# Two PSUM banks for the projections of mixer A, their evacuations two steps later, and one score bank fewer

## The chip, the cores and the metric

The kernel runs on all 8 cores of one Trainium2 chip, each core on 1024 of the 8192 tokens, with no exchange between cores. The time is the device time of the slowest core in microseconds (us); a result is the median over executions.

## The reference, cut to what matters

The program is one layer of a hybrid encoder: RMSNorm, a combined input projection, mixer A (dilated sliding-window attention, 8 heads of 128), mixer B (grouped-query attention over all tokens), an output projection, a product-key expert layer, and a last norm. The change touches mixer A alone:

```python
h = rms_norm(x, norm1_g[l])
proj = h @ w_in[l]
qa, ka, va, qb, kb, vb = jnp.split(proj, splits, axis=-1)
out_a = dilated_window_attention(qa_, ka_, va_)
...
# in dilated_window_attention, for each block of queries and three (window, dilation) branches:
sc = jnp.einsum('bhqd,bhqpkd->bhqpk', qblk, kg).astype(jnp.float32) * scale
sc = sc + bias[None, :, None]          # ALiBi
p = jnp.exp(sc - lse[..., None])
o = jnp.einsum('bhqpk,bhqpkd->bhqpd', p.astype(v.dtype), vg)
w = jax.nn.softmax(lse, axis=-1)       # the branches are joined by their denominators
```

The kernel computes it as one dense attention over a window of 3072 tokens, where a precomputed mask holds how often a key is hit by the branches, times the exponential of the ALiBi term.

## The kernel before, in words

Every operation goes through a small recorder (class Fw). Each engine executes its operations in the order in which they were recorded, and waits for the operations on which its own depend, by the names in r= and w=. ("ps", b) is PSUM bank b, of which there are eight (0 to 3 in psA, 4 to 7 in psB). There is no planner: the order of record is the order of execution.

The stages are: norm of the window, query projection of mixer B (bank 0, 1), mixer A, keys and values of mixer B, attention B, output projection, expert layer (the largest), last norm. A barrier of all engines stands between stages, so a stage starts when the one before has ended.

Mixer A works head by head. a2_loads (L374) fetches a head's weights WA and its mask. a2_proj_groups (L379) cuts a head's projections into 14 groups, each of which fills a bank of 128x512: six groups for the keys (L401, 16 matmuls of 512 columns), two for the queries (L407, the same) and six for the values (L414, 64 matmuls of 128 columns). A group of keys or queries is cut in four pieces of 4 matmuls, one of values in four pieces of 16: 56 pieces a head. All go to bank 0. Keys and queries are evacuated by ScalarE (L403, L410), values by VectorE (L417), and the evacuation is recorded right behind the last piece of its group.

Head 0's projections run alone, ahead of all attention. Those of head h+1 run between the steps of head h's attention, through hook: it is called once in each of a head's 40 steps (two chunks of 20 key tiles, one for each 512 queries), and records as many pieces as bring their count to 1.4 times the steps so far, so the steps bring 2, 1, 2, 1, 1 pieces, and so on. Head 7 has no projections beside it.

attention (L276 ff) with three score banks (sbanks 1, 2, 3) works with a lookahead of L = 2. Step i records on TensorE the scores qk(i+2) (L285, one matmul of 512 columns), on ScalarE the exponential of step i (L296), on VectorE the mask product of step i (L301), on TensorE pv(i) (L310 and L311: values and denominators, two matmuls of 512 columns), and then calls hook. At a chunk's end VectorE takes the reciprocal of the denominators (L315) and multiplies (L316). Mixer B uses the same function, with four banks and without mask and hook.

The lines that set the rhythm:

```python
L = nb - 1
...
if i + L < n:
    qk(i + L)
...
fw.op("pe", pv, r=[pid, vid, "ones"], w=[("ps", pso), ("ps", psd)])
if hook is not None:
    hook(i)
```

Of the kernel before, what the change touches and what calls it, by code (L numbers as in the profile page):

```python
# [10 lines left out]
BF16 = mybir.dt.bfloat16  # L11
U32 = mybir.dt.uint32
AF = mybir.ActivationFunctionType
# [112 lines left out]
def build_program():  # L126
    nc = bass.Bass("TRN2", target_bir_lowering=False)
    fw = Fw()
# [61 lines left out]
    ar = Ar()  # L190
# [84 lines left out]

    def attention(KT_fn, V_fn, QT, kts, kid, vid, qid, mask_fn, mask_id, E2, P2, rec, dst, dst_id, pso, psd, tagc,  # L276
                  sbanks=(2, 3), hook=None):
# [42 lines left out]
    hwin = ar.alloc([128, 16, WIN], BF16)  # L320
# [6 lines left out]
    for ck in range(WIN // 256):  # L327
        s = ck % 2
# [19 lines left out]
    win_ids = [("hwin", i) for i in range(6)]  # L348
    for tt in range(8):
        for half in range(2):  # L350
            def mm(e, tt=tt, half=half):
                ins = None
                for dk in range(16):
# [5 lines left out]
                                                           func=AF.Copy), r=[("ps", half)], w=["qraw"])  # L359
# [5 lines left out]
    WA = [ar.alloc([128, 16, 384], BF16) for _ in range(2)]  # L365
    maskS = [ar.alloc([128, 23, 128], BF16) for _ in range(2)]
    KT_h = [ar.alloc([128, WIN], BF16) for _ in range(2)]
    V_h = [ar.alloc([128, 24, 128], BF16) for _ in range(2)]
    QT_h = [ar.alloc([128, TOK], BF16) for _ in range(2)]
    E2 = [ar.alloc([128, 512], BF16) for _ in range(3)]  # L370
    P2 = [ar.alloc([128, 512], BF16) for _ in range(3)]
    rec = ar.alloc([128, 512])

    def a2_loads(h):  # L374
        s = h % 2
        fw.dma("gp", WA[s], wA[h].rearrange("(dk p) c -> p dk c", p=128), w=[("WA", s)])
        fw.dma("sp", maskS[s].rearrange("p a b -> p (a b)"), maskA[h], w=[("mask", s)])

    def a2_proj_groups(h):  # L379
        s = h % 2  # L380
        pieces = []

        def add_group(nmm, mk_mm, evac):
            per = 4 if nmm == 16 else 16
            for p0 in range(0, nmm, per):
                last = (p0 + per >= nmm)

                def piece(p0=p0, last=last):
                    def mm(e):
                        ins = None  # L390
                        for q in range(p0, p0 + per):
                            ins = mk_mm(e, q)
                        return ins
                    fw.op("pe", mm, r=[("WA", s)] + win_ids, w=[("ps", 0)])
                    if last:
                        evac()
                pieces.append(piece)

        for c6 in range(6):
            add_group(16,  # L400
                      lambda e, dk, c6=c6: e.matmul(bank(0), WA[s][:, dk, 128:256], hwin[:, dk, c6 * 512:(c6 + 1) * 512],  # L401
                                                    start=(dk == 0), stop=(dk == 15)),
                      lambda c6=c6: fw.op("act", lambda e: e.activation(out=KT_h[s][:, c6 * 512:(c6 + 1) * 512], in_=bank(0),  # L403
                                                                         func=AF.Copy), r=[("ps", 0)], w=[("KTh", s)]))
        for c2 in range(2):
            add_group(16,
                      lambda e, dk, c2=c2: e.matmul(bank(0), WA[s][:, dk, 0:128],  # L407
                                                    hwin[:, dk, 1024 + c2 * 512:1024 + (c2 + 1) * 512],
                                                    start=(dk == 0), stop=(dk == 15)),
                      lambda c2=c2: fw.op("act", lambda e: e.activation(out=QT_h[s][:, c2 * 512:(c2 + 1) * 512], in_=bank(0),  # L410
                                                                         func=AF.Copy), r=[("ps", 0)], w=[("QTh", s)]))
        for gg in range(6):
            add_group(64,
                      lambda e, q, gg=gg: e.matmul(bank(0)[:, (q // 16) * 128:(q // 16 + 1) * 128],  # L414
                                                   hwin[:, q % 16, (4 * gg + q // 16) * 128:(4 * gg + q // 16 + 1) * 128],
                                                   WA[s][:, q % 16, 256:384], start=(q % 16 == 0), stop=(q % 16 == 15)),
                      lambda gg=gg: fw.op("dve", lambda e: e.tensor_copy(  # L417
                          V_h[s][:, 4 * gg:4 * gg + 4, :].rearrange("p a b -> p (a b)"), bank(0)),
                          r=[("ps", 0)], w=[("Vh", s)]))
        return pieces  # L420

    a2_loads(0)
    for g in a2_proj_groups(0):
        g()
    for h in range(8):
        s = h % 2
        if h + 1 < 8:
            a2_loads(h + 1)
            pend = a2_proj_groups(h + 1)
        else:  # L430
            pend = []
        cnt_t = [0]
        npend = len(pend)

        def hook(i, pend=pend, cnt_t=cnt_t, npend=npend):
            cnt_t[0] += 1
            want = (npend * cnt_t[0] + 39) // 40
            while pend and (npend - len(pend)) < want:
                pend.pop(0)()
        for qc in range(2):  # L440
            kts = list(range(4 * qc, 4 * qc + 20))
            qt0 = 8 + 4 * qc
            pso, psd = (4, 5) if qc == 0 else (6, 7)

            def mask_fn(i, kts=kts, qt0=qt0, s=s):
                m0 = 11 - (kts[i] - qt0)
                return maskS[s][:, m0:m0 + 4, :].rearrange("p a b -> p (a b)")
            attention(lambda kt, s=s: KT_h[s][:, kt * 128:(kt + 1) * 128], lambda kt, s=s: V_h[s][:, kt, :],
                      QT_h[s][:, qc * 512:(qc + 1) * 512], kts, ("KTh", s), ("Vh", s), ("QTh", s), mask_fn, ("mask", s),
                      E2, P2, rec, mixA[:, h, qc * 512:(qc + 1) * 512], ("mixT", h), pso, psd, "A",  # L450
                      sbanks=(1, 2, 3), hook=hook)
        while pend:
            pend.pop(0)()
    fw.barrier()

    ar.p = P0
# [145 lines left out]
    mixB = ar.alloc([128, 8, TOK], BF16)  # L602
    E2 = [ar.alloc([128, 512], BF16) for _ in range(4)]
    rec = ar.alloc([128, 512])
    cnt = 0
    for h in range(8):
        kv = h // 4
        for qc in range(2):
# [18 lines left out]
    for oc in range(4):  # L627
        s = oc % 2
        fw.dma("gp", Wo[s], w_out3[:, :, oc * 512:(oc + 1) * 512], w=[("Wo", s)])
        for tt in range(8):  # L630
            b = k % 4
            k += 1

            def mm(e, tt=tt, s=s, b=b):
# [8 lines left out]
                r=[("ps", b), "acc"], w=["acc"])  # L643
# [15 lines left out]
    for tt in range(8):  # L659
# [33 lines left out]
    for piece in range(4):  # L693
        s = piece % 2
        fw.dma("gp", Wq[s], wq3[:, :, piece * 512:(piece + 1) * 512], w=[("Wq", s)])
        for bb in range(4):
            blk = piece * 4 + bb
            for half in range(2):
                b = k % 4
                k += 1  # L700

                def mm(e, bb=bb, half=half, s=s, b=b):
# [7 lines left out]
                    out=qT[:, blk, half * 512:(half + 1) * 512], in_=bank(b), func=AF.Copy), r=[("ps", b)], w=["qT"])  # L710
# [11 lines left out]
    pb = ar.alloc([128, 128], U32)  # L722
# [160 lines left out]
    for tt in range(8):  # L883
        onehot_prelude(tt)
        nxt = topk_stages(tt + 1) if tt + 1 < 8 else []
        for g in range(128 // NT):
            if g < len(nxt):
# [3 lines left out]
               r=[("Gs", tt % 2, tq_) for tq_ in range(0, 128, 4)], w=[("Gd", tt)], key=("Gdk", tt % 2))  # L891
# [10 lines left out]
           w=["acc"] + [("acc", t_, o_) for t_ in range(8) for o_ in range(4)], key="accld")  # L902
# [3 lines left out]
    for grp in range(128 // GRP):  # L906
        gsl = grp % 2
        for j in range(GRP):
# [5 lines left out]
                   r=all_gd, w=[("Gc", s3)])  # L914
            for half in range(2):
                b = kU % 2
                kU += 1

                def mm(e, s3=s3, half=half, b=b):
# [9 lines left out]
                    r=[("ge", b), ("Gc", s3)], w=[("AT", gsl, j)])  # L929
        for tt in range(8):  # L930
            for oc in range(4):
                b = 4 + (kV % 4)
                kV += 1

                def vm(e, gsl=gsl, tt=tt, oc=oc, b=b):
# [8 lines left out]
                    r=[("ps", b), ("acc", tt, oc)], w=[("acc", tt, oc)], extra=None)  # L944
# [11 lines left out]
    for tt in range(8):  # L956
        s = tt % 2
# [7 lines left out]
              r=[("rsf", tt), "gf"], w=[("ost", s)])  # L965
# [82 lines left out]
```

How the kernel before makes its waits and increments, by code:

```python
            def body(e, mine=mine, final=final):  # L103
                seen = {}
                for o in mine:
                    for j in sorted(o["deps"]):
                        k, v = self.ops[j]["sig"]
                        if seen.get(k, 0) >= v:
                            continue
                        seen[k] = v
                        e.wait_ge(sems[k], v)
                    if o["fn"] is None:
                        continue
                    ins = o["fn"](e)
                    if o["signal"]:
                        k, v = o["sig"]
                        ins.then_inc(sems[k], 16 if o["dma"] else 1)
                if final is not None:
                    for k, v in sorted(final.items(), key=str):
                        if k[0] == "k" and seen.get(k, 0) < v:
                            e.wait_ge(sems[k], v)
```

## Time and profile before

| | us |
|---|---|
| median of 3 runs | 5597.22 (5590.62 to 5888.88) |
| profiled execution, its own time | 5602.27 |
| profiled execution, span of the slowest core (core 2) | 5600.7 |
| spans of all cores | 5557.3 to 5600.7 |
| mixer A on core 2: projections of head 0 | 442.6 to 506.7 |
| mixer A on core 2: attention of heads 0 to 7 | 506.7 to about 1320 |
| TensorE busy over the span | 3926.2 (70%) |
| VectorE busy over the span | 2332.9 (42%) |
| ScalarE busy over the span | 1555.9 (28%) |

The profile is of one execution, on the slowest core. Every position below is in us from the start of the span. PE is TensorE's matmuls, PEld its weight loads, DVE is VectorE, ACT is ScalarE. The ends of matmuls are modelled: those of a row of matmuls overlap the next start, so the distance of two starts is the time that a matmul takes of the engine, and a listed idle time is shorter than the pause between them by the overlap.

### The profile page before, as it was taken

The page shows a single profiled execution, that of the slowest core. Times are in us where ns is not written, and L with a number is a line of the kernel's source. Part 1 is how long each engine was busy: PE and PEld are TensorE (multiplying, and loading weights), DVE is VectorE, ACT ScalarE, POOL GpSimd, SP SyncE. Part 2 cuts the span into 40 slices and gives each one's busy share as a digit, 9 for nine tenths or more (in the row PEclk, how much of TensorE's full clock was granted, in tenths as well). Part 3 has the DMA queues.
Part 4 walks back from the last instruction along what each step waited for, and adds up shares of the span by engine and source line. Part 5 has one row for each costly group of instructions (what it writes and reads, how often), then busy time and mean ns, then how long its engine had stood idle before and what let it go on. Part 6 is the DMA issues. An engine that isn't in the chain of part 4 may idle for free.

```text
span 5600.7 us, 66235 instructions; the slowest of 8 cores (5557.3 to 5600.7 us)
## 1 busy us (share of the span) xinstructions
PE 3926.2 (70%) x21336; PEld 1894.4 (34%) x21336; DVE 2332.9 (42%) x4103; ACT 1555.9 (28%) x2416; POOL 509.6 (9%) x359
## 2 busy tenths in 40 slices
PE   1246777775666999968631111139999999999997
PEld 1113444342333444423211111114444444444443
DVE  4341333334333010002069899835353444444444
ACT  2111222224666888851212121110100000000001
POOL 0000000000000000000014444420000000000000
PEclk8568999997888999989765555569999999999998
DMA  5302011004553000034400100154545445454544
GB/s 136 79 0 45 18 31 21 17 7 116 168 160 98 1 1 1 1 82 106 64 1 30 60 31 30 60 150 82 100 89 94 95 89 100 85 104 80 109 76 115
DMA packets 306814, 382.78 MB, mean 68 GB/s; under 512 B 139440, under 2 KB 262704, under 8 KB 302896
## 3 DMA queue, kind: packets, MB, share of 16 engines
q0 software_dynamic: 72240, 168.35, 17.1%
q1 hardware_dynamic: 234240, 210.21, 13.2%
q8 instruction: 182, 2.98, 0.2%
q14 instruction: 152, 1.25, 0.1%
HBM read 496.52 MB, written 50.33 MB: 98 GB/s over the span
## 4 chain that ended last, share of the span: by engine, by line
PE 66%; DVE 12%; issue 7%; ACT 5%; DMA 5%; POOL 3%; another core or an unknown queue 1%; DVEq 0%; ACTq 0%; SPq 0%; POOLq 0%
PE psB L938 16%; PE psA L922 16%; PE psB L310 6%; PE psB L311 5%; PE psA L285 5%; PE psA L521 3%; PE psA L401 3%; PE psA L414 3%; DVE arena L862 2%; DMA arena<-xT 2%; PE psA L705 2%; PE psA L637 2%; POOL arena L864 2%; PE psA L354 1%; DVE arena L860 1%
## 5 line engine op out<-in xcount | busy, mean ns | idle before, releaser
L922 PE MATMUL psA<-arena 128*128 128x512 bf16 x4096 | 893.1, 380 | 55.1 <-DMA arena<-UT_l 47.1
L938 PE MATMUL psB<-arena 128*128 128x512 bf16 x4096 | 889.2, 379 | 43.8 <-DVE arena L927 43.8
L296 ACT ACTIVATE arena<-psA 128x512 bf16<-128x512 f32 x1344 | 778.7, 599 | 306.6 <-PE psA L285 257.6
L942 DVE TENSOR_TENSOR arena<-psB,arena 128x512 f32<-128x512 f32 x1024 | 706.6, 691 | 212.8 <-PE psB L938 211.4
L310 PE MATMUL psB<-arena 128*128 128x512 bf16 x1344 | 516.5, 384 | 171.1 <-DVE arena L301 165.1
L926 ACT ACTIVATE arena<-psA 128x512 bf16<-128x512 f32 x256 | 152.8, 597 | 1641.3 <-PE psA L922 1622.2
L872 PE MATMUL psB<-arena 128*128 128x128 bf16 x1024 | 133.5, 303 | 647.6 <-POOL arena L864 545.2
L922 PEld LDWEIGHTS psA<-arena 128*128 128x128 bf16 x4096 | 401.3, 98 | 541.5 <-issue 60.9
L938 PEld LDWEIGHTS psB<-arena 128*128 128x128 bf16 x4096 | 398.5, 98 | 534.5 <-issue 58.6
L311 PE MATMUL psB<-arena 128*128 128x512 bf16 x1344 | 516.5, 384 | 0.0
L285 PE MATMUL psA<-arena 128*128 128x512 bf16 x1344 | 502.1, 383 | 1.0 <-DVE arena L584 1.0
L927 DVE TENSOR_TENSOR arena<-arena 128x512 bf16<-128x512 bf16 x256 | 108.9, 425 | 854.9 <-ACT arena L926 769.8
L315 DVE RECIPROCAL arena<-psB 128x512 f32<-128x512 f32 x32 | 107.4, 3356 | 635.5 <-PE psB L311 635.5
L301 DVE SCALAR_TENSOR_TENSOR arena<-arena 128x512 bf16<-128x512 bf16 x320 | 223.8, 746 | 301.3 <-ACT arena L296 299.1
L872 PEld LDWEIGHTS psB<-arena 128*128 128x128 bf16 x1024 | 94.1, 132 | 686.9 <-issue 677.9
L877 ACT ACTIVATE arena<-psB 128x512 bf16<-128x512 f32 x256 | 139.0, 595 | 631.4 <-PE psB L872 631.2
L864 POOL TENSOR_TENSOR arena<-arena 128x2048 bf16<-128x2048 f32 x64 | 265.4, 4146 | 452.7 <-DVE arena L862 434.1
L310 PEld LDWEIGHTS psB<-arena 128*128 128x128 bf16 x1344 | 132.4, 99 | 364.8 <-issue 234.8
L521 PE MATMUL psA<-arena 128*128 128x512 bf16 x768 | 207.3, 435 | 41.4 <-ACT arena L528 37.7
L401 PE MATMUL psA<-arena 128*128 128x512 bf16 x768 | 207.3, 408 | 35.5 <-DMA arena<-wA 19.6
L41 POOL DMA_DIRECT2D arena<-UT_l x128 | 67.8, 530 | 1689.6 <-PE psA L922 1671.7
L414 PE MATMUL psA<-arena 128*128 128x128 bf16 x3072 | 194.1, 219 | 18.0 <-DVE arena L417 11.3
(147 smaller groups left out, 3414.4 us busy)
## 6 DMA issues: line engine op xcount, KB each, us to landing
arena<-xT SPq DMA_DIRECT2D x44, 2048.0 KB, 13.3
arena<-UT_l POOLq DMA_DIRECT2D x128, 512.0 KB, 7.3
arena<-V_l POOLq DMA_DIRECT2D x128, 512.0 KB, 9.6
Gd<-arena SPq DMA_DIRECT2D x8, 4096.0 KB, 11.6
arena<-Gd SPq DMA_DIRECT2D x128, 256.0 KB, 10.5
arena<-wA POOLq DMA_DIRECT2D x8, 1536.0 KB, 11.7
arena<-x_own SPq DMA_DIRECT2D x1, 8192.0 KB, 35.0
arena<-w_out POOLq DMA_DIRECT2D x4, 2048.0 KB, 27.9
```

The source lines that it names most:

```text
L285: fw.op("pe", lambda e, kt=kt, b=b: e.matmul(bank(b), KT_fn(kt), QT, start=True, stop=True), r=[kid, qid], w=[("ps", b)])
L296: fw.op("act", lambda e, b=b, Eb=Eb: e.activation(out=Eb, in_=bank(b), func=AF.Exp, scale=SCALE), r=[("ps", b)], w=[("E", i % nb)])
L310: e.matmul(bank(pso), V_fn(kt), Pb, start=(i == 0), stop=(i == n - 1))
L311: return e.matmul(bank(psd), ones_bf, Pb, start=(i == 0), stop=(i == n - 1))
L401: lambda e, dk, c6=c6: e.matmul(bank(0), WA[s][:, dk, 128:256], hwin[:, dk, c6 * 512:(c6 + 1) * 512], start=(dk == 0), stop=(dk == 15)),
L414: lambda e, q, gg=gg: e.matmul(bank(0)[:, (q // 16) * 128:(q // 16 + 1) * 128], hwin[:, q % 16, (4 * gg + q // 16) * 128:(4 * gg + q // 16 ...
L521: ins = e.matmul(bank(bb), xb[s][:, dk, sub * 128:(sub + 1) * 128], Wkv[:, dk, :], start=(dk == 0), stop=(dk == 15))
L864: fw.op("gp", lambda e: e.tensor_tensor(A1[s], A1t[s], RT[:, 2, t0:t0 + NT].unsqueeze(2).to_broadcast([128, NT, 128]), ALU.mult), r=["RT", ...
L872: ins = e.matmul(bank(b)[:, j * 128:(j + 1) * 128], A1[s][:, 4 * q4 + j, :], A2[s][:, 4 * q4 + j, :], start=True, stop=True)
L922: ins = e.matmul(bank(b), UT[s3][:, dk, :], h2T[:, dk, half * 512:(half + 1) * 512], start=(dk == 0), stop=(dk == 15))
L938: ins = e.matmul(bank(b), AT[gsl][:, j, tt * 128:(tt + 1) * 128], Vc[gsl][j][:, oc * 512:(oc + 1) * 512], start=(j == 0), stop=(j == GRP - 1))
L942: fw.op("dve", lambda e, tt=tt, oc=oc, b=b: e.tensor_tensor(acc[:, tt, oc * 512:(oc + 1) * 512], bank(b), acc[:, tt, oc * 512:(oc + 1) * 5 ...
```

## The change

Projections alternate between banks 0 and 1, by the number of the group in its head (pb). Each piece now comes as a pair of the piece and, for the last of a group, its evacuation. In the attention of a head, hook does not record the evacuation behind its piece: it puts it on the list late, with the present step plus 2, and records it at the start of the call of hook in that step, ahead of that step's pieces. What is left on the list when the head's attention has been recorded is recorded then, behind the last reciprocal and product. Head 0's own projections are evacuated at once as before, but in alternating banks. Bank 1 was a score bank: mixer A's attention has two, (2, 3), which makes L = 1, and two buffers each for E2 and P2 in place of three.

```diff
-    E2 = [ar.alloc([128, 512], BF16) for _ in range(3)]
-    P2 = [ar.alloc([128, 512], BF16) for _ in range(3)]
+    E2 = [ar.alloc([128, 512], BF16) for _ in range(2)]
+    P2 = [ar.alloc([128, 512], BF16) for _ in range(2)]
...
+        gcount = [0]
 
         def add_group(nmm, mk_mm, evac):
             per = 4 if nmm == 16 else 16
+            pb = gcount[0] % 2
+            gcount[0] += 1
...
-                    fw.op("pe", mm, r=[("WA", s)] + win_ids, w=[("ps", 0)])
-                    if last:
-                        evac()
-                pieces.append(piece)
+                    fw.op("pe", mm, r=[("WA", s)] + win_ids, w=[("ps", pb)])
+                pieces.append((piece, (lambda pb=pb: evac(pb)) if last else None))
...
     a2_loads(0)
-    for g in a2_proj_groups(0):
-        g()
+    for (pc, ev) in a2_proj_groups(0):
+        pc()
+        if ev is not None:
+            ev()
...
+        late = []
+
+        def hook(i, pend=pend, cnt_t=cnt_t, npend=npend, late=late):
             cnt_t[0] += 1
+            for (d, ev) in [x for x in late if x[0] <= cnt_t[0]]:
+                ev()
+            late[:] = [x for x in late if x[0] > cnt_t[0]]
             want = (npend * cnt_t[0] + 39) // 40
             while pend and (npend - len(pend)) < want:
-                pend.pop(0)()
+                pc, ev = pend.pop(0)
+                pc()
+                if ev is not None:
+                    late.append((cnt_t[0] + 2, ev))
...
-                      sbanks=(1, 2, 3), hook=hook)
+                      sbanks=(2, 3), hook=hook)
         while pend:
-            pend.pop(0)()
+            pc, ev = pend.pop(0)
+            pc()
+            if ev is not None:
+                late.append((0, ev))
+        for (d, ev) in late:
+            ev()
+        late[:] = []
```

The matmuls and evacuations of the groups are the same as before, with bank(pb) for bank(0).

## Rows read from the trace of the kernel before

**Rows 1.** The page, chain that ended last, shares of the span by line

```profile
PE psB L938 16%; PE psA L922 16%; PE psB L310 6%; PE psB L311 5%; PE psA L285 5%; PE psA L521 3%; PE psA L401 3%; PE psA L414 3%; DVE arena L862 2%; DMA arena<-xT 2%; PE psA L705 2%; PE psA L637 2%; POOL arena L864 2%; PE psA L354 1%; DVE arena L860 1%
```

**Rows 2.** Stretches (PE, PEld, DVE, ACT, POOL, PEclk, DMA): a head; later stage

```profile
613.69:722.72 109.03, 83.29 (x632) 46.12 (x632) 39.44 (x52) 26.18 (x49) 1.14 (x2) 0.94 0.13 22
...
1330.00:1640.00 310.00, 196.30 (x1454) 95.39 (x1455) 101.01 (x164) 189.56 (x156) 0.00 (x0) 0.79 0.61 168
```

**Rows 3.** Timeline of PE, projections of head 0 (start, us, what, idle before)

```profile
453.08 3.61 PE L401 MATMUL psA<-arena 128*128 128x512 bf16 x16 [0.84 <-ACT arena L403]
...
484.47 3.73 PE L414 MATMUL psA<-arena 128*128 128x128 bf16 x64 [0.94 <-DVE arena L417]
489.14 3.73 PE L414 MATMUL psA<-arena 128*128 128x128 bf16 x64 [0.94 <-DVE arena L417]
```

**Rows 4.** Timeline of all engines around one evacuation of keys, head 0

```profile
529.89 0.60 ACT L403 ACTIVATE arena<-psA 128x512 bf16<-128x512 f32 x1 [4.44 <-PE psA L401]
530.39 1.57 ACT L296 ACTIVATE arena<-psA 128x512 bf16<-128x512 f32 x3
531.08 2.08 DVE L301 SCALAR_TENSOR_TENSOR arena<-arena 128x512 bf16<-128x512 bf16 x3 [4.59 <-ACT arena L296]
531.98 0.38 PE L310 MATMUL psB<-arena 128*128 128x512 bf16 x1 [1.97 <-DVE arena L301]
...
532.41 1.02 PE L401 MATMUL psA<-arena 128*128 128x512 bf16 x4
533.27 0.38 PE L285 MATMUL psA<-arena 128*128 128x512 bf16 x1
```

**Rows 5.** Timeline, head 6: undisturbed step with a piece of values; a stall

```profile
1231.01 0.38 PE L285 MATMUL psA<-arena 128*128 128x512 bf16 x1
...
1231.48 0.60 ACT L296 ACTIVATE arena<-psA 128x512 bf16<-128x512 f32 x1 [1.18 <-PE psA L285]
...
1232.55 0.38 PE L285 MATMUL psA<-arena 128*128 128x512 bf16 x1
...
1241.82 0.38 PE L310 MATMUL psB<-arena 128*128 128x512 bf16 x1 [1.39 <-DVE arena L301]
```

**Rows 6.** Waits of the period 613.69 to 722.72: us in total, times, longest

```profile
PE psB L310 <- DVE arena L301: 22.0, 10, 5.0
```

**Rows 7.** Chunk's end and head's end, head 0: PE timeline, reciprocals, CAST's source view

```profile
560.19 0.38 PE L311 MATMUL psB<-arena 128*128 128x512 bf16 x1
...
565.63 0.59 PE L310 MATMUL psB<-arena 128*128 128x512 bf16 x1 [3.56 <-DVE arena L301]
...
569.25 0.38 PE L285 MATMUL psA<-arena 128*128 128x512 bf16 x1
...
611.71 0.38 PE L311 MATMUL psB<-arena 128*128 128x512 bf16 x1
...
618.64 0.58 PE L310 MATMUL psB<-arena 128*128 128x512 bf16 x1 [5.02 <-DVE arena L301]
...
622.86 0.57 PE L285 MATMUL psA<-arena 128*128 128x512 bf16 x1
...
560.67 3.36 DVE L315 RECIPROCAL arena<-psB 128x512 f32<-128x512 f32 x1 [2.97 <-PE psB L311]
613.69 3.35 DVE L315 RECIPROCAL arena<-psB 128x512 f32<-128x512 f32 x1
...
L417 DVE CAST arena<-psA x48: 690/691/693, 483.6 to 1268.2; 128x512 bf16<-128x512 f32 x48
```

**Rows 8.** Timeline, head 7: a step at the lower clock, and the two last reciprocals

```profile
1274.51 0.63 PE L285 MATMUL psA<-arena 128*128 128x512 bf16 x1
...
1275.24 0.60 ACT L296 ACTIVATE arena<-psA 128x512 bf16<-128x512 f32 x1 [5.31 <-PE psA L285]
...
1291.92 3.36 DVE L315 RECIPROCAL arena<-psB 128x512 f32<-128x512 f32 x1 [0.84 <-PE psB L311]
1315.42 3.36 DVE L315 RECIPROCAL arena<-psB 128x512 f32<-128x512 f32 x1 [0.84 <-PE psB L311]
```

More of the change, by code:

```diff
@@ L381, in a2_proj_groups, with piece @@
         pieces = []
+        gcount = [0]
         def add_group(nmm, mk_mm, evac):
             per = 4 if nmm == 16 else 16
+            pb = gcount[0] % 2
+            gcount[0] += 1
             for p0 in range(0, nmm, per):
                 last = (p0 + per >= nmm)
-                def piece(p0=p0, last=last):
+                def piece(p0=p0, pb=pb):
                     def mm(e):
@@ L391, in mm @@
                         for q in range(p0, p0 + per):
-                            ins = mk_mm(e, q)
+                            ins = mk_mm(e, q, pb)
                         return ins
-                    fw.op("pe", mm, r=[("WA", s)] + win_ids, w=[("ps", 0)])
-                    if last:
-                        evac()
-                pieces.append(piece)
+                    fw.op("pe", mm, r=[("WA", s)] + win_ids, w=[("ps", pb)])
+                pieces.append((piece, (lambda pb=pb: evac(pb)) if last else None))
@@ L399, in a2_proj_groups @@
         for c6 in range(6):
             add_group(16,
[L401 to L404, printed above, removed]
+                      lambda e, dk, pb, c6=c6: e.matmul(bank(pb), WA[s][:, dk, 128:256], hwin[:, dk, c6 * 512:(c6 + 1) * 512],
+                                                        start=(dk == 0), stop=(dk == 15)),
@@ L405, in a2_proj_groups @@
+                      lambda pb, c6=c6: fw.op("act", lambda e: e.activation(out=KT_h[s][:, c6 * 512:(c6 + 1) * 512], in_=bank(pb),
+                                                                             func=AF.Copy), r=[("ps", pb)], w=[("KTh", s)]))
         for c2 in range(2):
             add_group(16,
-                      lambda e, dk, c2=c2: e.matmul(bank(0), WA[s][:, dk, 0:128],
-                                                    hwin[:, dk, 1024 + c2 * 512:1024 + (c2 + 1) * 512],
-                                                    start=(dk == 0), stop=(dk == 15)),
@@ L410, in a2_proj_groups @@
-                      lambda c2=c2: fw.op("act", lambda e: e.activation(out=QT_h[s][:, c2 * 512:(c2 + 1) * 512], in_=bank(0),
-                                                                         func=AF.Copy), r=[("ps", 0)], w=[("QTh", s)]))
+                      lambda e, dk, pb, c2=c2: e.matmul(bank(pb), WA[s][:, dk, 0:128],
+                                                        hwin[:, dk, 1024 + c2 * 512:1024 + (c2 + 1) * 512],
+                                                        start=(dk == 0), stop=(dk == 15)),
@@ L412, in a2_proj_groups @@
+                      lambda pb, c2=c2: fw.op("act", lambda e: e.activation(out=QT_h[s][:, c2 * 512:(c2 + 1) * 512], in_=bank(pb),
+                                                                             func=AF.Copy), r=[("ps", pb)], w=[("QTh", s)]))
         for gg in range(6):
             add_group(64,
-                      lambda e, q, gg=gg: e.matmul(bank(0)[:, (q // 16) * 128:(q // 16 + 1) * 128],
-                                                   hwin[:, q % 16, (4 * gg + q // 16) * 128:(4 * gg + q // 16 + 1) * 128],
-                                                   WA[s][:, q % 16, 256:384], start=(q % 16 == 0), stop=(q % 16 == 15)),
@@ L417, in a2_proj_groups @@
-                      lambda gg=gg: fw.op("dve", lambda e: e.tensor_copy(
-                          V_h[s][:, 4 * gg:4 * gg + 4, :].rearrange("p a b -> p (a b)"), bank(0)),
-                          r=[("ps", 0)], w=[("Vh", s)]))
+                      lambda e, q, pb, gg=gg: e.matmul(bank(pb)[:, (q // 16) * 128:(q // 16 + 1) * 128],
+                                                       hwin[:, q % 16, (4 * gg + q // 16) * 128:(4 * gg + q // 16 + 1) * 128],
+                                                       WA[s][:, q % 16, 256:384], start=(q % 16 == 0), stop=(q % 16 == 15)),
@@ L420, in a2_proj_groups @@
+                      lambda pb, gg=gg: fw.op("dve", lambda e: e.tensor_copy(
+                          V_h[s][:, 4 * gg:4 * gg + 4, :].rearrange("p a b -> p (a b)"), bank(pb)),
+                          r=[("ps", pb)], w=[("Vh", s)]))
         return pieces
     a2_loads(0)
-    for g in a2_proj_groups(0):
-        g()
+    for (pc, ev) in a2_proj_groups(0):
+        pc()
+        if ev is not None:
+            ev()
     for h in range(8):
@@ L433, in build_program @@
         npend = len(pend)
-        def hook(i, pend=pend, cnt_t=cnt_t, npend=npend):
+        late = []
+        def hook(i, pend=pend, cnt_t=cnt_t, npend=npend, late=late):
             cnt_t[0] += 1
+            for (d, ev) in [x for x in late if x[0] <= cnt_t[0]]:
+                ev()
+            late[:] = [x for x in late if x[0] > cnt_t[0]]
             want = (npend * cnt_t[0] + 39) // 40
             while pend and (npend - len(pend)) < want:
-                pend.pop(0)()
+                pc, ev = pend.pop(0)
+                pc()
+                if ev is not None:
+                    late.append((cnt_t[0] + 2, ev))
         for qc in range(2):
```

## The prediction

> **What bounds the kernel now.** I read the page first: its chain, the work that ended last, is mostly TensorE's, and the lines of mixer A that stand in it (L310, L311, L285, L401, L414; the first three shared with mixer B) sum to 23% of the span [rows 1]. Mixer A is about a sixth of the span, so even a large gain there moves the whole by a few per cent. Since a barrier ends the stage, what it saves arrives at the end in full, and nothing outside it is touched.
>
> Next the busy time by stretch. From one head's last reciprocal to the next's, 109.03 us pass; heads 1 to 6 repeat this within 0.5 us. In it VectorE is busy 39.4 us, ScalarE 26.2, and TensorE 83.3 by modelled ends [rows 2]. What TensorE's work takes when nothing stops it comes from the distance of starts: 4 matmuls of 512 columns take 0.86 us (0.215 each), pv's two take 0.43 [rows 4], and an undisturbed step with one piece of values takes 1.54 [rows 5], so that the piece is 1.54 - 0.645 = 0.895. A head has 40 qk (8.6 us), 80 matmuls of pv (17.2), 128 of keys and queries (27.6), and 24 pieces of values (21.4): 74.8 us. So 34 us of each head are not work. TensorE is the engine that sets the time, and it is late for three reasons.
>
> One: the evacuation. With one bank, ScalarE's queue holds it between two exponentials, where it waits until the group's last matmul is done. The next exponential comes behind it, then the mask product, then pv: 1.97 us of TensorE lost [rows 4]; for values, VectorE's CAST does the same at 1.39 [rows 5]. Where the next group starts in the same call of hook, TensorE waits for the evacuation itself, 0.84 or 0.94 as in head 0's projections [rows 3]. Two: a chunk's end, where the reciprocal of 3.36 us and the product hold up the next chunk's first mask product (3.56 and 5.02 us idle) [rows 7]. Three: TensorE's clock, granted at 0.94 over the period [rows 2]; behind such pauses it runs for some microseconds at the lower of its levels (1.2 in place of 2.4 GHz).
> The waits of the period for a mask product sum to 22.0 us [rows 6]. The two chunk ends are 8.6 of them, and the evacuations the other 13.4.
>
> **The change part by part.** I do not subtract stalls but build a head's new length, since the new stalls differ in kind.
>
> *Head 0's projections.* The group after next needs the evacuation, and that is 3.4 us away while the evacuation takes 0.6 to 0.7. All 13 pauses between groups go. A pause is 0.84 idle plus the overlap of ends (3.61 - 16 x 0.215 = 0.17), so 1.01, for the 8 that an ACT evacuation causes; for values it is 4.67 between starts less 4 x 0.895, so 1.09, for 5 [rows 3]. Gain 8 x 1.01 + 5 x 1.09 = 13.5 us. What is late next is TensorE's own work.
>
> *Deferred evacuations.* Recorded two steps later, they find their group done and no longer wait. They keep their 0.6 and 0.7 us and need a hole in their queue: exponentials start at least 1.5 us apart and take 0.5 to 0.6, mask products 0.67 to 0.75, and CAST 0.69 [rows 4, 5, 7]. Mask product and CAST together are 1.36 to 1.44, within the shortest step's 1.51. So I cost them at nothing; without that cover a value evacuation would cost at most its 0.69, six times a head, 4 us. The bank's next group starts five pieces later, three or four steps, so it finds the bank free. Bound: none to all of the six groups late, 0 to 4 us a head; I take 0, as the hole is in the rows.
>
> *One score bank fewer.* This is the price. From the start of a qk to the start of its pv the path is 0.47 to the exponential (1231.01 to 1231.48) [rows 5], 0.69 from there to the mask product and 0.90 from that to pv [rows 4]: 2.05 us (rounded down; the three roundings go one way). With L = 2 two steps lay between. With L = 1 TensorE has between the two only pv (0.43), the step's pieces, and the next qk (0.215). One piece of keys: 1.51 us, so a stall of 2.05 - 0.215 - 1.51 = 0.33. One piece of values: 0.30. Two pieces: 2.37, none. A step that follows a stalled one has 0.33 more distance, so its successor does not stall. With pieces 2, 1, 2, 1, 1, two steps of five stall: 16 a head, less two that fall into the chunk starts. The last step of each chunk, which has no qk to issue, stalls 0.215 more. Sum: 7 x 0.33 + 0.55 and 6 x 0.30 + 0.30 + 0.52 = 5.5 us a head. Bounds: nothing, if an engine answers faster, to 0.33 in each of the 24 single-piece steps plus the ends, 8.4.
>
> *Chunk's end.* In a head's middle, pv's last start 560.19 plus 0.215 to pv's next start 565.63 is 5.22 us, all VectorE's and unchanged. TensorE has one piece (0.86) and now qk twice (0.43) in it: 3.93 idle. At a head's end it is 611.93 to 618.64, 6.72 us, because the reciprocal stands behind the last CAST: it starts 1.98 after pv's start, where the middle one starts 0.48 after it [rows 7]. Now the CAST is recorded behind reciprocal and product, and holds up the next mask product by 0.6 to 0.7 instead. 6.72 - 1.50 + 0.61 = 5.83, less 0.895 and 0.43 of work: 4.50 idle.
>
> *Clock.* Behind the middle pause the first pv and its 8 matmuls last from 565.63 to 569.25, 3.62 where 2.15 is their time at the upper level, and 622.86 - 618.64 is 4.22 [rows 7]. With what follows I take 1.7 and 2.2, 3.9 a head. Work (74.8) and waits for mask products (22.0) leave 12.2 of the 109.0 us; four pauses of 1.01 and 1.09 between groups are some 4 of it, my two dips 3.9, and the other 4 are small delays behind evacuations and a dip in the keys' part behind stalls of 1.97. I take these as gone with their cause. Bounds: 3.9 to 8.
>
> *A head's new length:* 74.8 + 5.5 + 3.9 + 4.5 + 3.9 = 92.6 us for 109.1. Seven heads have this form: 7 x 16.5 = 115.5 us gained.
>
> *Head 7, no projections beside it.* Its chunks now take 23.50 us (reciprocal at 1291.92 to 1315.42) [rows 8]. With L = 1, two steps take a path and a pv: 2.05 + 0.43 = 2.48, so 1.24 a step. At the lower clock the first part of the path is 0.73 for 0.47 [rows 8], pv 0.85, and two steps 3.16. Four steps low, sixteen high, plus the unchanged 5.2 of the chunk's end: 30.3 us. That is 6.8 more a chunk; I take 14 for both. If the clock stays low throughout: 35.8, so 25 for both.
>
> The weights' load is issued a head ahead and the mask's at a head's start, both past queues that carry nothing else here; at 93 us a head both still land in time.
>
> **Sum:** 13.5 + 115.5 - 14 = 115 us. The profiled execution took 5602.3 us by its own time, 1.6 above its span, so 5487; it lies 5 above the median of the runs. The metric goes by the median: 5597.2 - 115 = **5482 us**, a gain of 2.05%.
>
> **A rule weighed.** The stalls of 1.39 us [rows 5] come every 7 us in the values' part, and the trace keeps the upper level there; behind pauses of 3.6 and 5.0 it shows the lower [rows 7]. The Trainium skill ("TensorE: Matmul & The Clock Gate", section "A second HAM failure mode: psum-queue depth-cycling") tells of another kernel in which cycling through PSUM banks each iteration left TensorE small idles between groups so often that its clock oscillated. By that rule the change, which trades a few long pauses for many of 0.3 us, could lose at the clock what it gains in pauses; by the rows it does not. What the rule would do here is the second rival.
>
> **The rivals.**
> *Half of the gain goes into lookahead.* The path is longer than 2.05 us while evacuations are in the queues, all 24 single-piece steps stall by 0.33 (2.9 more a head), the clock costs 1.6 a head more than I take, and head 7 runs at the lower clock (11 more). Gain 115 - 7 x 4.5 - 11 = 72: 5525 us. For it: the hole for CAST is only 0.1 wide, and head 7's TensorE would be busy 0.645 in 1.24. Against: after a stalled step the rows leave 0.33 of slack, and from the lower level the engine is busy 1.28 in 1.58.
> *Slower: the short stalls hold the clock down.* In heads 0 to 6 the steps that stall come every 3 to 5 us. Each 512-column matmul at the lower level costs 0.21 more; all 248 of a head are 52 us. The gain of a head, 16.5, is used up when 78 of them, about a third, run low beyond those of today; if all did, the seven heads would lose 7 x (52 - 16.5), 250 us, and the time would be about 5850. For it: in the stretch behind mixer A, where TensorE is busy 196 of 310 us, the mean granted clock is 0.79 [rows 2]. Against: in steps with a stall TensorE would still be busy over 80%, and stalls of 1.39 did not do it.
> *It does not do what it says.* If the evacuations still delayed exponentials (the deferral being too short), the heads would lose 5.5 each on top of today, head 7 14, and only 13.5 would be won: 5597 + 39 = 5636, within 2%. For it speaks little, since the group's end is then two steps, 3 us, in the past.
>
> **How the numbers follow.** My forecast has 0.65 (5460 to 5510), the first rival 0.24 (5510 to 5545), the slower clock 0.05, no effect 0.06. 2% is about what a measurement of this kernel can tell from no change, and that line, 5485, runs through my forecast: of its 0.65 some 0.5 lies below. So faster by over 2%: 0.50; within 2%: 0.45; slower: 0.05. The range takes in the first rival's middle and, below, a head without new stalls or with the shorter dips (another 5.5 x 0.5 x 7 = 20): 5460 to 5532.
>
> **What would show it.** Right: head 0's 14 groups without pauses, some 50 us for 64; reciprocals of successive heads 92 to 93 us apart; waits of pv for the mask product of 0.15 to 0.4 us at single-piece steps, none of 1.97 or 1.39; no wait of a piece for an evacuation; the last reciprocal of head h ahead of its CAST; head 7's reciprocals 30 apart. Wrong: waits of L401 or L414 for an evacuation, a granted clock below 0.94 in the heads, a head's period of 97 or more, or head 7's above 33.

## The result, and the profile after

Of the ten executions of each kernel half or more (five of the changed kernel, six of before) ran at a lower granted clock on one or both dies and took over 5650 us, which puts the medians over all ten at 5569.3 us for the changed kernel and 5831.7 for before, so the comparison takes the others alone. The ratio of those is 0.9781 (95% interval 0.9759 to 0.9803): the changed kernel is 2.2% faster. They took 5473.8 to 5484.4 us with the change, and 5590.6 to 5614.3 before.

In the profile of the changed kernel I read core 2, which is also the core of the rows of before; its granted clock over the span is 0.850, for 0.852 there. Its span is 5459.6 us for 5600.7. First where the 141 us are. The last reciprocal of mixer A starts at 1175.57 for 1315.42, and from there to the end of the span it is 4284.0 us for 4285.3: all of it lies before the end of mixer A. Mixer A's first projection starts at 417.33 for 442.68, though nothing ahead of it was changed. That start differs nearly as much between kernels whose first stages are alike: 410.3 in e1, 430.4 in e4 (both below). So I take lengths from the first projection to the last reciprocal: 758.2 us for 872.7, which is 114.5 less.

Busy time by stretch, changed kernel, core 2: head 0's projections, three periods from a head's last reciprocal to the next head's, and head 7's two chunks (columns as in [rows 2]).

```profile
417.30:471.80 54.50, 51.71 (x515) 34.58 (x516) 5.07 (x8) 7.14 (x11) 1.14 (x1) 0.96 0.20 25
558.37:650.81 92.44, 81.24 (x636) 45.27 (x634) 41.40 (x51) 27.57 (x48) 1.14 (x1) 0.96 0.15 27
...
835.08:928.76 93.68, 82.24 (x636) 45.60 (x633) 41.40 (x51) 27.57 (x48) 1.15 (x1) 0.95 0.15 26
1114.83:1145.07 30.24, 18.08 (x77) 5.47 (x73) 19.48 (x23) 11.83 (x20) 0.00 (x0) 0.94 0.00 1
1145.07:1175.57 30.50, 18.05 (x60) 4.70 (x58) 18.89 (x22) 11.83 (x20) 0.00 (x0) 0.89 0.00 1
```

A period is 92.4 us where it was 109.03 [rows 2]. VectorE is busy 41.4 us of it and ScalarE 27.6, where they had 39.4 and 26.2: no work left them, it only stands elsewhere in their queues. TensorE's timeline, in head 0's projections and in attention:

```profile
417.33 22.91 PE L402 MATMUL psA<-arena 128*128 128x512 bf16 x96 [18.50 <-DMA arena<-wA]
440.08 7.07 PE L408 MATMUL psA<-arena 128*128 128x512 bf16 x32
446.99 21.60 PE L415 MATMUL psA<-arena 128*128 128x128 bf16 x384
468.43 0.59 PE L285 MATMUL psA<-arena 128*128 128x512 bf16 x2
...
541.41 0.38 PE L310 MATMUL psB<-arena 128*128 128x512 bf16 x1
541.63 0.38 PE L311 MATMUL psB<-arena 128*128 128x512 bf16 x1
541.84 1.06 PE L415 MATMUL psA<-arena 128*128 128x128 bf16 x16
542.74 0.38 PE L285 MATMUL psA<-arena 128*128 128x512 bf16 x1
543.27 0.38 PE L310 MATMUL psB<-arena 128*128 128x512 bf16 x1 [0.15 <-DVE arena L301]
```

The 14 groups, 512 matmuls, now run without a pause between them; each of these pauses was a line with 0.84 or 0.94 us of idle time [rows 3]. In attention a step with one piece ends in a short wait for the mask product. The 0.15 us stand beside the overlap of ends; by starts, pv comes 0.53 after its qk where an undisturbed one comes 0.21 after it, so 0.32 us are lost. One step of the keys' part of a 93.7 us head lost 0.70 (at 861.10, 0.53 listed), and I have no cause for that. All waits of TensorE in the period 558.37 to 650.81 are one row:

```profile
PE psB L310 <- DVE arena L301: 11.1, 17, 4.3
```

It was 22.0 us in 10 waits [rows 6]. Of the 17, two are the chunk ends (8.1 us) and 15 the short ones. No piece waits for an evacuation any more. A head's end, all engines:

```profile
557.89 0.38 PE L311 MATMUL psB<-arena 128*128 128x512 bf16 x1
558.11 1.05 PE L415 MATMUL psA<-arena 128*128 128x128 bf16 x16
558.37 3.36 DVE L315 RECIPROCAL arena<-psB 128x512 f32<-128x512 f32 x1 [0.84 <-PE psB L311]
559.00 0.59 PE L285 MATMUL psA<-arena 128*128 128x512 bf16 x2
...
561.84 0.69 DVE L316 TENSOR_TENSOR arena<-psB,arena 128x512 bf16<-128x512 f32 x1
562.44 0.68 DVE L418 CAST arena<-psA 128x512 bf16<-128x512 f32 x1
563.04 1.41 DVE L301 SCALAR_TENSOR_TENSOR arena<-arena 128x512 bf16<-128x512 bf16 x2
563.93 0.38 PE L310 MATMUL psB<-arena 128*128 128x512 bf16 x1 [4.34 <-DVE arena L301]
```

The reciprocal starts 0.48 us after the last pv's start, where it was 1.98 [rows 7], and the CAST follows behind the product. The pause is still there, and so is the spell of the lower clock behind it.

### The profile page after: what moved, and what is told of

It reads as the page before. It is cut to its first block, busy times and chain, and to the rows that moved or that the text cites. A ratio compares the mean times of both kernels' runs of the same rounds, so it can differ in the third digit from the quotient of the medians.

```text
span 5571.8 us, 66398 instructions; the slowest of 8 cores (5454.1 to 5571.8 us)
## 1 busy us (share of the span) xinstructions
PE 4009.9 (72%) x21336; PEld 1911.0 (34%) x21336; DVE 2348.1 (42%) x4103; ACT 1566.1 (28%) x2416; POOL 509.6 (9%) x359
## 4 chain that ended last, share of the span: by engine, by line
PE 65%; DVE 13%; issue 7%; ACT 6%; DMA 5%; POOL 3%; another core or an unknown queue 1%; DVEq 0%; ACTq 0%; SPq 0%; POOLq 0%
PE psB L954 17%; PE psA L938 17%; PE psB L310 5%; PE psB L311 5%; PE psA L285 5%; PE psA L537 3%; PE psA L402 2%; DVE arena L878 2%; PE psA L415 2%; PE psA L653 2%; PE psA L721 2%; DMA arena<-xT 2%; DVE arena L301 2%; POOL arena L880 2%; ACT arena L296 2%
## 5 line engine op out<-in xcount | busy, mean ns | idle before, releaser
L938 PE MATMUL psA<-arena 128*128 128x512 bf16 x4096 | 948.0, 396 | 58.1 <-DMA arena<-UT_l 49.5
L954 PE MATMUL psB<-arena 128*128 128x512 bf16 x4096 | 932.9, 392 | 43.8 <-DVE arena L943 43.8
L938 PEld LDWEIGHTS psA<-arena 128*128 128x128 bf16 x4096 | 414.1, 101 | 586.5 <-issue 244.6
L310 PE MATMUL psB<-arena 128*128 128x512 bf16 x1344 | 514.5, 383 | 105.3 <-DVE arena L301 101.5
L311 PE MATMUL psB<-arena 128*128 128x512 bf16 x1344 | 515.1, 383 | 0.0
L285 PE MATMUL psA<-arena 128*128 128x512 bf16 x1344 | 504.1, 383 | 1.0 <-DVE arena L600 1.0
L301 DVE SCALAR_TENSOR_TENSOR arena<-arena 128x512 bf16<-128x512 bf16 x320 | 238.9, 751 | 369.9 <-ACT arena L296 304.0
L315 DVE RECIPROCAL arena<-psB 128x512 f32<-128x512 f32 x32 | 107.5, 3358 | 623.3 <-PE psB L311 623.3
L537 PE MATMUL psA<-arena 128*128 128x512 bf16 x768 | 203.6, 430 | 44.0 <-ACT arena L544 37.8
L402 PE MATMUL psA<-arena 128*128 128x512 bf16 x768 | 196.5, 396 | 22.0 <-DMA arena<-wA 22.0
L415 PEld LDWEIGHTS psA<-arena 128*128 128x128 bf16 x3072 | 182.0, 98 | 30.1
## 6 DMA issues: line engine op xcount, KB each, us to landing
Gd<-arena SPq DMA_DIRECT2D x8, 4096.0 KB, 11.1
```

Source lines behind the costliest of these rows:

```text
L301: fw.op("dve", lambda e, Pb=Pb, Eb=Eb, mk=mk, kt=kt: e.scalar_tensor_tensor(out=Pb, in0=Eb, scalar=validT[:, kt:kt + 1], in1=mk, op0=ALU.m ...
L310: e.matmul(bank(pso), V_fn(kt), Pb, start=(i == 0), stop=(i == n - 1))
L311: return e.matmul(bank(psd), ones_bf, Pb, start=(i == 0), stop=(i == n - 1))
L402: lambda e, dk, pb, c6=c6: e.matmul(bank(pb), WA[s][:, dk, 128:256], hwin[:, dk, c6 * 512:(c6 + 1) * 512], start=(dk == 0), stop=(dk == 15)),
L415: lambda e, q, pb, gg=gg: e.matmul(bank(pb)[:, (q // 16) * 128:(q // 16 + 1) * 128], hwin[:, q % 16, (4 * gg + q // 16) * 128:(4 * gg + q ...
L537: ins = e.matmul(bank(bb), xb[s][:, dk, sub * 128:(sub + 1) * 128], Wkv[:, dk, :], start=(dk == 0), stop=(dk == 15))
```

## The experiments

The theory: a head's time is TensorE's work plus pauses that can be counted one by one; the deferral removes those of evacuations, lookahead 1 adds short ones, and the chunk ends stay. The rivals: the second projection bank carries the gain; the short stalls are no matter of lookahead; the clock follows the short stalls. All lengths are of core 2, a head's period from the last reciprocal of one head to that of the next.

| kernel | projection banks | evacuation | score banks | head, us | head 7's second chunk, us | mixer A, us |
|---|---|---|---|---|---|---|
| before | 1 | at once | 3 | 109.0 to 109.6 | 23.5 | 872.7 |
| e3 | 1 | at once | 2 | 113.9 to 114.7 | 30.6 | 922.2 |
| e9 | 2 | at once | 3 | 109.0 to 109.6 | 22.6 | 859.7 |
| e2 | 2 | at once | 2 | 111.0 to 114.6 | 30.9 | 899.4 |
| changed | 2 | two steps late | 2 | 92.1 to 93.8 | 30.5 | 758.2 |
| e7 | 2 | one step late | 2 | 93.8 to 93.9 | 30.5 | 763.7 |
| e4 | 2 | two steps late | 3 | 86.7 to 87.4 | 23.5 | 706.2 |
| e10 | 2, pieces in chunk starts | two steps late | 2 | 82.2 to 83.2 | 30.4 | 687.2 |
| e5 | 2, pieces in chunk starts | two steps late | 3 | 76.06 | 22.9 | 627.4 |

### e1: alternating banks in head 0's projections alone

```diff
-            pb = gcount[0] % 2
+            pb = gcount[0] % 2 if h == 0 else 0
...
-                    late.append((cnt_t[0] + 2, ev))
+                    ev()
...
-                      sbanks=(2, 3), hook=hook)
+                      sbanks=(1, 2, 3), hook=hook)
```

(The changed kernel, set back so in its heads; E2 and P2 have three buffers again.)

> The kernel before with alternating banks in head 0's own projections alone (64 us there before). Step by step reckoning: the 13 pauses between its groups go, 13.5 us, and the heads keep their 109.1 us, head 7 its 23.5 a chunk: mixer A 13.5 us shorter than before, no more. Rival (the second bank carries most of the gain): a head's period falls too, which this kernel can't show unless something of the first part reaches the heads. Rival on the clock: an unbroken run of projections brings the granted clock down, so that less than 10 us is won.

Mixer A took 861.6 us, 11.2 less than before; the heads kept 109.0 to 109.6. TensorE's timeline shows why it is 11 and not 13:

```profile
440.65 21.60 PE L415 MATMUL psA<-arena 128*128 128x128 bf16 x384
463.41 0.59 PE L285 MATMUL psA<-arena 128*128 128x512 bf16 x2 [1.16 <-DVE arena L418]
```

Bank 1 is a score bank in this kernel, and the last group of values lies in it, so the first qk waits 1.16 us for that evacuation. The changed kernel has no such wait. Another 0.7 us went at the start, where the key matmuls took 23.4 us for the 22.75 of the changed kernel. More than 10 us were won, so the rival on the clock does not hold; on the second bank in the heads this run says nothing, as expected, and e9 has to.

### e9 and e2: the second bank with evacuations recorded at once

e2 is the changed kernel with this, and e9 is e4 (below) with it:

```diff
-                    late.append((cnt_t[0] + 2, ev))
+                    ev()
```

> Two projection banks, three score banks, lookahead 2, and every evacuation recorded at once: against the kernel before this differs by the second projection bank alone. My theory (the second bank only removes the wait inside a call of hook, and the exponential behind the evacuation is late anyway): 107.5 to 109 us a head for 109.1. Rival (the second bank carries a good part of the heads' gain): below 103.

> The changed kernel with each evacuation recorded right behind its group again, in the heads too; two banks and lookahead 1 stay. My theory (the deferral carries the gain, since the wait sits in ScalarE's and VectorE's queues ahead of the next exponential or mask product): the stalls of 1.97 and 1.39 us come back and a head's period is 107 to 110 us in place of 92.4. Rival (the second bank carries the gain, since TensorE's next group no longer waits for the bank): the period stays below 97 us.

e9 has 109.13 us where before has 109.03, a little above the 107.5 to 109 that I expected: in the heads the second bank alone is worth nothing. Its timeline, where a group ends inside a call of hook and TensorE goes straight on to the other bank:

```profile
595.50 1.89 PE L402 MATMUL psA<-arena 128*128 128x512 bf16 x8
596.62 0.60 ACT L404 ACTIVATE arena<-psA 128x512 bf16<-128x512 f32 x1 [4.59 <-PE psA L402]
597.11 1.08 ACT L296 ACTIVATE arena<-psA 128x512 bf16<-128x512 f32 x2
597.22 0.38 PE L285 MATMUL psB<-arena 128*128 128x512 bf16 x1
597.81 1.41 DVE L301 SCALAR_TENSOR_TENSOR arena<-arena 128x512 bf16<-128x512 bf16 x2 [4.58 <-ACT arena L296]
598.70 0.38 PE L310 MATMUL psB<-arena 128*128 128x512 bf16 x1 [1.10 <-DVE arena L301]
```

The 0.84 us wait for the bank is gone, and 1.10 us are lost a moment later, because the exponential stood behind the evacuation in ScalarE's queue all the same. The wait moved from the bank to the queue. The sums of a period say the same. TensorE's waits before, beside the 22.0 us of [rows 6], and then all of them in e9:

```profile
PE psA L401 <- ACT arena L403: 1.7, 2, 0.8
PE psA L414 <- DVE arena L417: 0.9, 1, 0.9
PE psA L414 <- ACT arena L410: 0.8, 1, 0.8
```

```profile
PE psB L310 <- DVE arena L301: 25.8, 14, 5.0
```

The four waits for the bank are 3.4 us, and 22.0 + 3.4 is 25.4, where e9 has 25.8. In e2 the heads took 111 to 115 us. I had expected 107 to 110; the direction is the theory's, and my size was up to 5 us too low. One period of 112.2 us has these waits:

```profile
PE psB L310 <- DVE arena L301: 28.7, 21, 5.2
```

That is 3.3 us more than before, and the period is 3.2 longer; TensorE's busy time (83.2 us) and its granted clock (0.94) are those of before. The step from e2 to the changed kernel, 112.8 to 92.7 us in the mean, is the deferral alone. Whether the deferral would do it with a single projection bank no run shows.

### e3: the kernel before with two score banks

```diff
-    E2 = [ar.alloc([128, 512], BF16) for _ in range(3)]
-    P2 = [ar.alloc([128, 512], BF16) for _ in range(3)]
+    E2 = [ar.alloc([128, 512], BF16) for _ in range(2)]
+    P2 = [ar.alloc([128, 512], BF16) for _ in range(2)]
...
-                      sbanks=(1, 2, 3), hook=hook)
+                      sbanks=(2, 3), hook=hook)
```

> The kernel before with two score banks and two E2 and P2 buffers, and nothing else: the price of the lookahead by itself, beside evacuations at once. My theory: head 7, which has no projections, takes 30.3 us a chunk for 23.5; the other heads lose less than the 5.5 us that I reckoned for the changed kernel, because a stall of 1.97 gives the next step its slack: 110 to 113 us a head. Rival (the queue orders, not the lookahead, set the heads): 109 us a head and head 7 below 26 a chunk.

114 us a head, 30.1 and 30.6 for head 7's chunks: head 7 as expected, the heads 1 to 2 above. I had expected a loss below the 5.5 us of the changed kernel and it was 5, so the slack that I thought a stall gives was hardly there. Of the 4.9 us that the first period is longer than before, 2.7 are waits (28.1 us for 25.4) and 1.6 busy time, at a granted clock of 0.93 for 0.94. The lookahead has its price wherever the evacuations stand.

### e4: three score banks with the change

```diff
-    E2 = [ar.alloc([128, 512], BF16) for _ in range(2)]
-    P2 = [ar.alloc([128, 512], BF16) for _ in range(2)]
+    E2 = [ar.alloc([128, 512], BF16) for _ in range(3)]
+    P2 = [ar.alloc([128, 512], BF16) for _ in range(3)]
...
-            pso, psd = (4, 5) if qc == 0 else (6, 7)
+            pso, psd = (4, 5)
...
-                      sbanks=(2, 3), hook=hook)
+                      sbanks=(2, 3, 6), hook=hook)
```

> The changed kernel with three score banks (2, 3, 6) and three E2 and P2 buffers again, paid for by using one pair of banks (4, 5) for both chunks' values and denominators, which costs nothing by my reading, as the next chunk's first mask product stands behind the product that reads them. My theory: the stalls of single-piece steps go, 5.5 us a head, and head 7 is back at 23.5 a chunk: period 86 to 87.5 us in place of 92.4, mixer A some 52 us shorter than the changed kernel. Rival (the short stalls are the latency of deferred evacuations in the queues, not of the lookahead): period above 91. Rival (the shared pair of banks makes pv wait for the product): chunk ends longer than 5.2 us, period 90 or more.

The heads took 86.7 to 87.4 us, 5.7 less in the mean than the changed kernel's 92.7, head 7's chunks 23.8 and 23.5, mixer A 52.0 us less. One execution of the whole took 5440.4 us. TensorE's waits of a period:

```profile
PE psB L310 <- DVE arena L301: 7.7, 2, 4.1
```

Only the two chunk ends are left, and sharing one pair of banks made neither longer. The short stalls were the lookahead's, and both rivals fall.

### e7: one step late

```diff
-                    late.append((cnt_t[0] + 2, ev))
+                    late.append((cnt_t[0] + 1, ev))
```

> The changed kernel with evacuations one step late in place of two. My theory: one step is enough, because the group's last matmul ends before the next step's exponential has left the queue; the evacuation then waits a little and delays the following exponential by some 0.1 us: a head's period 92.4 to 94 us. Rival (the group's end is still waited for in the queue): 100 us or more.

93.8 to 93.9 us a head, as expected. TensorE's waits for the mask product sum to 11.6 us in 17 (11.1 in 17 with two steps), and its busy time is 82.2, as in those heads of the changed kernel that took 93.7 (82.24 us, granted clock 0.95). So most of the difference to the heads of 92.1 us goes with longer low spells of the clock and not with waits; whether the shorter deferral shifts these spells was not tried apart. One step is enough to get the evacuation out of the way.

### e5, e8, e10, e11: pieces kept for the chunk starts

```diff
+            if i == 0 and fill is not None:
+                fill()
...
-            want = (npend * cnt_t[0] + 39) // 40
+            want = ((npend - 2 * FILL) * cnt_t[0] + 39) // 40 + FILL * filled[0]
...
+        def fill():
+            filled[0] += 1
+            for _ in range(min(FILL, len(pend))):
+                take()
```

FILL is 4. fill is called behind a chunk's first qk's and ahead of its first pv. take records a piece as hook did, and first a late evacuation of the same bank, should there be one. e5 is e4 with this, e8 is the changed kernel with it, e10 repeats e8 and e11 repeats e5.

> Three score banks as in e4, and eight of a head's 56 pieces kept for its two chunk starts: four each are recorded between the first qk's and the first pv, where TensorE waits some 4 us for the reciprocal; the other 48 stay in the steps (1.2 a step). My theory: the pause at a chunk's end is filled (5.22 less 0.86, 0.65 and 3.44 leaves 0.3 us; 5.83 leaves 0.9), and without a pause the clock does not fall behind it (3.9 us a head): 76.5 to 79 us a head for e4's 87.0, mixer A some 60 us shorter than e4's 706, and the ratio to before near 0.96. Rival (the pause moves to the steps, since pieces taken out of them leave VectorE's mask products bare, or the clock falls for another reason): 83 us or more a head.

76.06 us a head in every head, below the 76.5 to 79 that I expected, and mixer A is 78.8 us shorter than e4's where I had some 60. Busy time of one period, and under it TensorE's waits in it, e5:

```profile
553.23:629.29 76.06, 75.29 (x636) 45.59 (x633) 41.58 (x51) 27.58 (x48) 1.14 (x1) 1.00 0.18 32
```

```profile
PE psB L312 <- DVE arena L303: 0.7, 1, 0.7
```

Here 74.8 us are the work that I counted at the upper clock, and 1.3 is all else. The granted clock is 1.00 where e4 has 0.94: with the pauses gone, the low spells behind them are gone too. From e4 to e5 a head loses 11 us: 7.0 of waits, and the rest clock and overlap of ends.

> The changed kernel, lookahead 1, with the pieces kept for the chunk starts as in e5. If the stalls of single-piece steps and the chunk ends add up independently, as in my sum, a head takes 74.8 + 5.5 + 1.5 + up to 1 = 82 to 83.5 us for 92.4, and head 7 stays at 30.4 a chunk. If the mixture of steps matters more (32 of 40 steps now have one piece, and stalled steps follow each other), 86 or more. If the clock is brought down by the stalls themselves and not by the pauses, it stays at 0.96 and below in the heads and the gain is under 7.

On core 2 e8's heads took 89.0 to 92.1 us, which would refute my sum; but from 620 to 1000 us the granted clock of cores 2, 3, 6 and 7 is 0.81, neither of the two levels, and on cores 0, 1, 4 and 5, where it is 1.00 in that stretch, the same heads took 82.2 to 83.2 us. The kernel ran once more:

> The kernel of e8 once more, since the first execution was disturbed on both dies (matmuls of 0.437 us in the median for 0.379). As there: 82 to 83.5 us a head if the two costs add up independently; 86 or more if stalled steps do not have the slack that I gave them; head 7 at 30.4 a chunk.

82.2 to 83.2 us again, now on all eight cores: the two costs add up independently. Busy time and TensorE's waits of one period, e10:

```profile
563.47:645.66 82.19, 77.86 (x636) 44.11 (x633) 41.42 (x50) 27.79 (x48) 1.14 (x1) 1.00 0.17 30
```

```profile
PE psB L312 <- DVE arena L303: 4.3, 18, 0.9
```

This is also the test of the slower rival of the prediction. Its short stalls are as frequent as the changed kernel's, 18 waits in a head, and without the long pauses the clock is 1.00. The short stalls do not bring it down; with the pauses of 4 us among them it fell, and filling those took the fall away.

> The kernel of e5 once more, for an interval: 76.06 us a head again, the ratio to the kernel before 0.956 to 0.961 (mixer A 627 us for 873, so 245 us of 5597 less).

76.06 us a head again, mixer A 627.6 us. Chosen as in the result, the executions of this kernel took 5350.2 and 5362.0 us beside 5584.5 to 5590.9 of the kernel before (e5), and 5353.7 and 5355.6 beside 5603.0 (e11): 0.956 to 0.960 by single executions, for which I have no interval. It beats both kernels, the changed one by some 2%.

## Why the prediction was right, and where it was not

I take core 2's lengths for each term.

- *Head 0's projections, 13.5 us.* Measured 13.0: from the first projection to the first qk 51.1 us for 64.1. The engine starts at the lower clock in both. What that costs differs between executions: the first 96 matmuls of the changed kernel take 22.75 us, 2.1 more than 96 x 0.215, in e1 2.8 more, and before it was 1.5 (the first 16 took 5.94 to the next start, of which 1.01 is the pause and 3.44 the work). I had no term for it.
- *Seven heads, 115.5 us.* From the first qk to head 6's last reciprocal 646.4 us for 762.0, so 115.6. The mean of six periods is 92.7 for the 92.6 that I built up. Right, and not by errors that cancel: the terms below agree one by one, the clock as what is left.
- *Stalls of the lookahead, 5.5 us a head.* e4 removes them and gains 5.7. The waits are where they were placed: two in five steps, 0.32 to 0.35 us each, and at a chunk's last step 0.53 to 0.56.
- *Evacuations at nothing.* Right: no row of a wait for one. That the cover is enough is shown by the values' part, where the CAST stands in each hole of VectorE and the stalls are no longer than elsewhere.
- *Chunk ends, 3.9 and 4.5 us idle.* Listed 3.77 and 4.34 idle, which is 3.9 and 4.5 with the overlap of ends. e5 shows that these pauses and their clock are 11 us of a head.
- *Clock, 3.9 us a head.* No run measures this term apart. What is left of 92.7 us after 74.8 of work, 5.7, 3.9 and 4.5 is 3.8. The granted clock rose from 0.94 to 0.95 and 0.96, and heads with 93.7 us have longer low spells than those with 92.1. The dip in the keys' part went, as I had assumed without a row that shows it.
- *Head 7, 14 us lost.* Its two chunks take 60.7 us for 46.7: 14.1. The working on record does not give its 30.3 us a chunk, though: four steps of 1.58, sixteen of 1.24 and 5.2 are 31.4. Measured are 30.2 and 30.5.

Sum 13.0 + 115.6 - 14.1 = 114.5 us for the 115 predicted. By the comparison, 1 - 0.9781 of 5597.2 is 122.6 us, and 114.5 lies within its interval (110 to 135). In what bounds the kernel, the five lines of [rows 1] sum to 22% of the span and not 23%; nothing hangs on it. The medium gain of the first rival (72 us) is outside it, the slower clock is refuted by e10, and "no effect" by every row.

What failed is the last step, from the gain to a time. I took 5597.2, the median of the three runs shown, as the base of the new median, and a range of 5460 to 5532 that holds only doubts about the gain, with no term for how far executions of one kernel lie apart, though one of those three was at 5888.9. Over ten executions the median of before is 5831.7 us and not 5597.2, with six of them above 5770, and that of the changed kernel is 5569.3, above the range, with five above 5650. The spread of the three runs, 5.3%, is larger than the whole gain, and it stood nowhere in my range.

The other five, 5473.8 to 5484.4, have a median of 5482, which is my figure, and in that there is some luck. The same choice puts before at 5602 and not at 5597, so the gain is 120 us where I had 115: a base too low by 5 and a gain too small by 5 cancel. Mixer A accounts for 114.5; no run shows where the rest lies, and it is less than the 11 to 24 us over which those executions spread.

In e2 and e3 my sums for kernels with evacuations at once were 1 to 5 us a head too low. Most of what these heads lose against before is waits: in the periods read, the waits rise by 3.3 us and the period by 3.2 in e2; in e3 it is 2.7 of 4.9, and 1.6 more are busy time at a slightly lower clock. So the slack behind an evacuation's stall hid less of the short stalls than I had thought.

## What to carry to other kernels

A second buffer doesn't help while the instruction that frees the first stands in an in-order queue ahead of something urgent: move that instruction to where its input is long done, and look at the queue, not at the bank, for the wait. To forecast such a change, build the new length of one period from the distances of starts, with each pause named, rather than subtract waits; here that came within 0.2 us of 92.7. A resource taken for the new buffer has its own price (here a score bank, 52 us over mixer A), and it is worth looking for one that is held without need, as the second pair of value banks was. Then fill what pause is left with work that has no deadline.

## What the runs showed of the hardware that I had not expected

The low spells of TensorE's clock go with the long pauses, not with the number of short ones. With waits of at most 0.9 us, 18 in 82 us (e10), the granted clock was 1.00; with two pauses of 3.8 and 4.3 us among the same short ones it was 0.95 to 0.96 (changed kernel). Filling the two pauses of a head gave 11.0 us (e4 to e5), for the 8.0 that they are in e4 (7.7 listed). Pauses need not be that long, as e2's keys' part shows behind stalls of 1.10 and 1.97 us, where a qk takes 0.63 us and not 0.38:

```profile
611.60 0.38 PE L310 MATMUL psB<-arena 128*128 128x512 bf16 x1 [1.97 <-DVE arena L301]
...
613.12 0.63 PE L285 MATMUL psA<-arena 128*128 128x512 bf16 x1
```

How long a pause has to be for that no run shows.

The length of the first stages, with the same instructions, moved the start of mixer A on core 2 between 410.3 and 442.7 us from run to run, so two profiles' spans can differ by 32 us for nothing, a third of the gain here. The length of mixer A is steadier: on core 2 it was 627.4 and 627.6 us in e5 and e11, and before it lay between 872.2 and 875.0 on the eight cores.
